# Splitting the transposed probabilities: the PSUM copy on ScalarE, the fp32r rounding on GpSimd

## The chip, the cores and the metric

The kernel runs on one core of one Trainium2 chip. The metric is the device time of one execution in microseconds (us). The kernel before has a median of 3531.86 us over 3 runs.

## The reference

A trunk of two layers over 1024 tokens of width 1024. Each layer has a token mixer (a short gated convolution beside sparse attention) and an MLP. The change lies in the attention, which has 8 query heads in 2 key groups of 4, head size 64, and three branches whose outputs are added under gates:

```python
p_cmp = masked_softmax(s_cmp, cmp_mask)          # c: 63 compressed keys
o_cmp = einsum(p_cmp, vcmp)
...
p_sel = masked_softmax(s_sel, m_sel)             # s: 8 selected blocks of 64 keys, causal
o_sel = einsum(p_sel, v_sel)
p_w = masked_softmax(s_w, m_w)                   # w: window of the last 512 keys
o_w = einsum(p_w, v_w)
o = g[:, :, 0] * o_cmp + g[:, :, 1] * o_sel + g[:, :, 2] * o_w
```

## The kernel before

Everything is float32. A product on TensorE (PE) that needs float32 accuracy is split: one operand x is written as high + low, where high is x rounded to fp32r and low = x - high, and both halves are multiplied. One Fori loop runs over the two layers, so the attention stage stands twice in the trace (about 624 to 931 us, and about 2340 to 2647 us).

**Units.** The attention runs over query tiles of 128 rows from the last (7) to the first (0). For each tile and key group there is a w set and an s set, and each set has four units, one for each head. A unit is: scores on PE into PSUM (`lin`), the negated row maximum on VectorE (DVE, `negm`, L1538), the exponential on ScalarE (ACT, L1172, into `prob`). A w set has up to 5 key tiles, an s set has all key tiles up to the diagonal (8 for the last query tile). When the four exponentials of a set are made, DVE makes four factors (`factors`, L1526 and L1528) and GpSimd (POOL) multiplies the four `prob` rows in place (L711). Between the tiles stands a c unit for the compressed branch, with a chain of some 15 small DVE instructions (L1466 to L1517).

**Groups.** Once a set is scaled, its probabilities are turned, one key tile at a time. A group is four transposes on PE (L953, L948 for the c branch) into one of the two 512-word halves ("banks") of the PSUM tile `aux`; then the split into `pTH` (high) and `pTL` (low); then `values` (L967, L968), two matmuls of 512 columns into `pv`. There are 148 such groups a layer, and 4 more of kind "b" that carry the block choice and are copied by ACT alone.

**Steps.** All engines go through one list of steps in program order, one unit a step, and no engine takes a thing out of order:

- PE at step u: the scores of the unit after this one, then the transposes of the groups of step u (two a step where the sets are long), and after each group's transposes the values of the group three places back (`V_AFTER = 3`). In a step without groups it makes the values of all groups that are waiting (a flush).
- ACT at step u: the exponential of unit u, then the high copies of step u's groups.
- DVE at step u: the maximum of unit u, then the low parts of the groups of step u - 1, then factors and the c chain where there are some.
- POOL: only the scalings, set by set.

The split of one group reads the PSUM bank twice, and it is the second read, on DVE, that frees the bank:

```python
act.activation(pt("high", x, r), turned(x, r), ACT.Copy).then_inc(t_hi, 1)                 # L1188
...
dve.tensor_tensor(pt("low", x, r), turned(x, r), pt("high", x, r).bitcast(F32),            # L1544
                  ALU.subtract).then_inc(t_free[x["bank"]], 1)
```

The transposes of a group wait on PE until the group two before it has freed the bank (L940), and `values` wait for the same semaphore (L961). `pTH` and `pTL` have four slots each (`PT = 4`): three in region r_x, the fourth in r_raw. A `region` lays several lists of tensors over one piece of SBUF.

Of the kernel before, what the change touches and what calls it, by code (L numbers as in the profile page):

```python
# [14 lines left out]
F32 = mybir.dt.float32  # L15
# [7 lines left out]
P = 128  # L23
# [197 lines left out]
PT = 4  # L221
# [5 lines left out]
def trunk(nc, a, out):  # L227

    with ExitStack() as ctx:
# [14 lines left out]
        def sem(name):  # L244
# [4 lines left out]

        other = TILE_OF[("ua", 4)] % RAW  # L250
        before = [("before", [P, other * 1024], F32)] * (other > 0)
        (wraw,), pt_r = region("r_raw", RAW * 1024, [("wraw", [P, RAW, 1024], F32)],
                               before + [("pTH3", [P, 512], F32R), ("pTL3", [P, 512], F32R)])

        (whi, wlo), (prob3,) = region("r_w", 2 * SPL * 1024, [(n, [P, SPL, 1024], F32R) for n in ("whi", "wlo")],
                                      [("prob3", [P, HPG, SEQ], F32)])
        tmp = sb("tmp", [P, 2, SEQ])


        (xT,), (cosT, sinT, kcT, vcT, fbuf, ropes), (vw, vs, pTH, pTL, scm, psum4, negm, sums, cst, imp, top8, left, fac) = region(  # L260
            "r_x", KC * SEQ, [("xT", [P, KC, SEQ], F32)],
            [("cosT", [P, SEQ], F32), ("sinT", [P, SEQ], F32), ("kcT", [P, SEQ], F32), ("vcT", [P, SEQ], F32),
             ("fbuf", [P, 2, SEQ], F32), ("ropes", [P, 2, SEQ], F32)],
# [1 line left out]
             ("pTL", [P, PT - 1, 512], F32R), ("scm", [P, NH, 64], F32), ("psum4", [P, NKV, 65], F32),  # L265
             ("negm", [P, len(UNITS) - NT], F32), ("sums", [P, len(UNITS) - NT], F32), ("cst", [P, 3, NH], F32),
             ("imp", [P, NKV, NS], F32), ("top8", [P, NKV, 8], F32), ("left", [P, NKV, NS], F32),
             ("fac", [P, 2, HPG], F32)])

        (hH, hL), (atH, atL, prob), (_, _, stG, stM), (xin,) = region(  # L270
            "r_h", 2 * KC * SEQ, [("hH", [P, KC, SEQ], F32R), ("hL", [P, KC, SEQ], F32R)],
# [62 lines left out]
        def pt(kind, x, r=P):  # L334

            t = x["v_no"] % PT
            if t == PT - 1:
                return dict(high=pt_r[-2], low=pt_r[-1])[kind][0:r, :]
            return dict(high=pTH, low=pTL)[kind][0:r, t, :]

        def turned(x, r=P):

            return aux[0:r, x["bank"] * 512:(x["bank"] + 1) * 512]

        x_keep = nc.dram_tensor("x_keep", [P, KC, SEQ], F32).ap()
        rope_keep = nc.dram_tensor("rope_keep", [2, P, SEQ], F32).ap()
# [247 lines left out]
        hid_sig, hid_silu, cmp_done, cmp_made = (sem(s) for s in ("hid_sig", "hid_silu", "cmp_done", "cmp_made"))  # L594
        rope_sum, rope_hi, v_hi, vc_lo = (sem(s) for s in ("rope_sum", "rope_hi", "v_hi", "vc_lo"))
        f_made, p_scaled = sem("f_made"), sem("p_scaled")
        t_hi, fin_low, fin_sum, fin_lo = (sem(s) for s in ("t_hi", "fin_low", "fin_sum", "fin_lo"))
        s_done, max_made, exp_made = (sem(s) for s in ("s_done", "max_made", "exp_made"))
        c_in_made, c_exp, sel_made = (sem(s) for s in ("c_in_made", "c_exp", "sel_made"))
        c_gated, t_done, v_done, o_hi = (sem(s) for s in ("c_gated", "t_done", "v_done", "o_hi"))  # L600
# [66 lines left out]
        with nc.Fori(0, DEPTH) as layer:  # L667
            with nc.Block() as block:
# [31 lines left out]
                @block.gpsimd  # L700
                def _(pool):
                    def attention():


                        for u in range(len(STEPS)):
                            for st in SETS:
                                for i in range(HPG):
                                    if st["last"] + SCALED_AFTER[i] == u:
                                        pool.wait_ge(f_made, st["no"] + 1)
                                        p = prob_of(st["no"], i)[:, 0:st["n"]]  # L710
                                        pool.tensor_scalar(p, p, fac[:, st["no"] % 2, i:i + 1], 1.0, ALU.mult, ALU.mult).then_inc(p_scaled, 1)  # L711
                                        pool.wait_ge(p_scaled, HPG * st["no"] + i + 1)

                    for n, t in enumerate(TILES):
                        if t[0] != "split":
                            continue
                        s = SPLIT_NO[n]
                        if s:

                            pool.wait_ge(w_split, s)  # L720
                        if t[5][0] == ("ua", 0):
                            attention()

                            pool.wait_ge(t_done, END_GROUP[len(SETS) - 1]["no"] + 1)
                        pool.wait_ge(raw_in[n % RAW], IN_SLOT[n])
                        if s >= SPL:

                            before = [m for m in SPLIT_NO if SPLIT_NO[m] == s - SPL][0]
                            done(pool, TILES[before][5][-1])
                        pool.tensor_scalar(whi[:, s % SPL, :], wraw[:, n % RAW, :], 1.0, 1.0, ALU.mult, ALU.mult).then_inc(w_hi, 1)  # L730
                        pool.wait_ge(w_hi, s + 1)
                        pool.tensor_tensor(wlo[:, s % SPL, :], wraw[:, n % RAW, :], whi[:, s % SPL, :].bitcast(F32),  # L732
                                           ALU.subtract).then_inc(w_split, 1)

                @block.tensor
                def _(pe):
# [219 lines left out]
                    def values(x):  # L956

                        if x["first"] and NTH[x["qt"]]:

                            pe.wait_ge(fin_sum, 2 * (NKV * (NTH[x["qt"]] - 1) + x["g"] + 1))  # L960
                        pe.wait_ge(t_free[x["bank"]], x["no"] // 2 + 1)  # L961
                        r = SEEN[x["qt"]] if x["kind"] == "c" else P
                        if x["kind"] == "c":
                            v = vcmp[0:r, x["g"], :]
                        else:
                            v = (vw if x["set"]["b"] == "w" else vs)[:, x["key"], x["g"], :]
                        pe.matmul(pv[:, x["g"], :], v, pt("high", x, r), start=x["first"], stop=False)  # L967
                        pe.matmul(pv[:, x["g"], :], v, pt("low", x, r), start=False, stop=x["last"]).then_inc(v_done, 1)  # L968
# [53 lines left out]
                def _(act):  # L1022
# [134 lines left out]
                    for u, here in enumerate(STEPS):  # L1157
                        if u < len(UNITS) and UNITS[u][0] == "c":
                            nth, n = NTH[UNITS[u][1]], SEEN[UNITS[u][1]]
                            act.wait_ge(c_in_made, nth + 1)  # L1160
                            if nth:
                                act.wait_ge(c_gated, nth)
                            act.activation(cprob[:, :, 0:n], scm[:, :, 0:n], ACT.Exp).then_inc(c_exp, 1)
                        elif u < len(UNITS):
                            b, qt, g, i, no = UNITS[u]
                            m, st = SCORES_BEFORE[u], SETS[no]
                            if no >= PROBS and i == 0:

                                act.wait_ge(t_done, END_GROUP[no - PROBS]["no"] + 1)
                            act.wait_ge(max_made, m + 1)  # L1170
                            at = chunks(st)[0][2]
                            act.activation(prob_of(no, i)[:, 0:st["n"]], scores(u)[:, at:at + st["n"]], ACT.Exp,  # L1172
                                           bias=negm[:, m:m + 1], accum_out=sums[:, m:m + 1]).then_inc(exp_made, 1)
                        for x in here:
                            o = aux[:, x["bank"] * 512:(x["bank"] + 1) * 512]
                            act.wait_ge(t_done, x["no"] + 1)
                            if x["kind"] == "b":
                                if NTH[x["qt"]] >= 2:

                                    act.wait_ge(s_done, [s for s in SETS if s["qt"] == x["qt"] + 2][-1]["last"] + 1)  # L1180
                                for g in range(NKV):
                                    ins = act.activation(selT[0:NS, x["qt"] % 2, g, :], o[32 * g:32 * g + NS, 0:P], ACT.Copy)
                                ins.then_inc(t_free[x["bank"]], 1)
                            else:
                                r = SEEN[x["qt"]] if x["kind"] == "c" else P
                                if x["v_no"] >= PT:
                                    act.wait_ge(v_done, x["v_no"] - PT + 1)
                                act.activation(pt("high", x, r), turned(x, r), ACT.Copy).then_inc(t_hi, 1)  # L1188
                        for st in SETS:
                            if st["b"] != "s":  # L1190
                                continue
                            k = NKV * NTH[st["qt"]] + st["g"]
                            if st["fin"] == u:

                                act.wait_ge(v_done, END_GROUP[st["no"]]["v_no"] + 1)
                                if k:
                                    act.wait_ge(fin_sum, 2 * k)
                                act.activation(low_half, pv[HD:P, st["g"], :], ACT.Copy).then_inc(fin_low, 1)
                            if st["fin"] + 2 == u:
                                act.wait_ge(fin_sum, 2 * (k + 1))  # L1200
                                act.activation(atH[:, 2 * st["g"]:2 * st["g"] + 2, st["qt"] * P:(st["qt"] + 1) * P],
                                               att.rearrange("p (j t) -> p j t", j=2), ACT.Copy).then_inc(o_hi, 1)
# [53 lines left out]
                def _(dve):  # L1256
# [273 lines left out]
                    for u in range(len(STEPS)):  # L1530
# [8 lines left out]
                        for x in STEPS[u - 1] if u else []:  # L1539
                            if x["kind"] != "b":  # L1540

                                r = SEEN[x["qt"]] if x["kind"] == "c" else P
                                dve.wait_ge(t_hi, x["v_no"] + 1)
                                dve.tensor_tensor(pt("low", x, r), turned(x, r), pt("high", x, r).bitcast(F32),  # L1544
                                                  ALU.subtract).then_inc(t_free[x["bank"]], 1)
                        for st in SETS:
                            if st["last"] + 1 == u:
                                factors(st)
# [164 lines left out]
```

## Time and profile before

| | |
|---|---|
| median of 3 runs | 3531.86 us (3531.05 to 3535.02) |
| time of the profiled execution | 3531.86 us |
| its span in the trace | 3530.1 us |
| busy over the span: PE, DVE, ACT, POOL | 94%, 52%, 22%, 32% |
| the low parts L1544, both layers | 296 instructions, 198.3 us, mean 686 ns |
| the scalings L711, both layers | 256 instructions, 182.6 us, mean 713 ns |

The shares are means over stages of very different kinds. Outside the attention PE works through dense products at 98 to 100% of a slice and the other engines wait for it. The attention is the part in which four engines pass work to each other, and the rows below are from there. A bracket behind an instruction in a timeline is the idle time of its engine before it, and what ended it.

### The profile page before, as it was taken

How to read it: one execution, taken by the hardware profiler on the slowest of the kernel's cores; microseconds unless marked ns; L12 is line 12 of the kernel's file. 1: busy time of each engine (PE TensorE's matmuls, PEld its weight loads, DVE VectorE, ACT ScalarE, POOL GpSimd, SP SyncE). 2: the span in 40 equal slices, each digit the busy share in tenths (PEclk: the TensorE clock that was granted, in tenths of full speed). 3: DMA queues.
4: the chain of work that ended last, by engine and by line, in shares of the span. 5: the costliest groups of instructions: out<-in, count | busy, mean ns of one | idle time of the engine just before them, and what ended most of it. 6: DMA issues, size and time to landing. Idle time of an engine off the chain costs nothing. (4 is left out here: it accounts for less than half of the span.)

```text
span 3530.1 us, 39234 instructions
## 1 busy us (share of the span) xinstructions
PE 3308.0 (94%) x15575; PEld 2687.7 (76%) x15605; DVE 1830.5 (52%) x1877; ACT 781.0 (22%) x1283; POOL 1119.9 (32%) x800
## 2 busy tenths in 40 slices
PE   4999999898898999999979999989979899999998
PEld 3788887676687888888868888767658788888887
DVE  7754344787636444333365443568865564433333
ACT  2100012666312000000120001147661210000002
POOL 3333322233332333333323333222333233333331
PEclk6999999999899999999989999999999999999999
DMA  5434431000422222111133343300005132211111
GB/s 166 147 96 131 138 96 48 1 1 1 157 66 66 72 72 68 52 48 48 36 122 96 113 137 111 81 7 1 1 9 195 37 96 72 72 48 48 48 48 60
DMA packets 349011, 256.92 MB, mean 73 GB/s; under 512 B 9500, under 2 KB 335506, under 8 KB 348563
## 3 DMA queue, kind: packets, MB, share of 16 engines
q1 hardware_dynamic: 334642, 209.75, 20.3%
q10 hardware_dynamic: 14177, 44.56, 3.4%
q8 instruction: 126, 2.06, 0.2%
q14 instruction: 66, 0.54, 0.0%
HBM read 223.87 MB, written 30.41 MB: 72 GB/s over the span
## 5 line engine op out<-in xcount | busy, mean ns | idle before, releaser
L730 POOL TENSOR_SCALAR whi<-wraw 128x1024 fp32r<-128x1024 f32 x238 | 266.2, 1119 | 1848.7 <-PE lin L759 1246.0
L759 PE MATMUL lin<-hH,whi 128*128 128x512 f32 x2272 | 719.1, 398 | 43.5 <-POOL wlo L732 35.4
L759 PE MATMUL lin<-hL,whi 128*128 128x512 f32 x2272 | 705.8, 392 | 0.0
L759 PE MATMUL lin<-hH,wlo 128*128 128x512 f32 x2272 | 705.2, 392 | 0.0
L732 POOL TENSOR_TENSOR wlo<-wraw,whi 128x1024 fp32r<-128x1024 f32 x238 | 644.2, 2707 | 19.9
L759 PEld LDWEIGHTS lin<-hH,whi 128*128 128x128 f32 x2272 | 423.9, 190 | 136.5 <-POOL wlo L732 39.5
L759 PEld LDWEIGHTS lin<-hL,whi 128*128 128x128 f32 x2272 | 430.5, 189 | 90.9
L759 PEld LDWEIGHTS lin<-hH,wlo 128*128 128x128 f32 x2272 | 429.9, 189 | 90.1
L1600 DVE SCALAR_TENSOR_TENSOR xT<-lin,adac,xT 128x1024 f32<-128x1024 f32 x144 | 184.8, 1283 | 542.3 <-PE lin L759 541.9
L711 POOL TENSOR_SCALAR prob<-prob,fac 128x640 f32<-128x640 f32 (+7 forms) x256 | 182.6, 713 | 471.2 <-DVE fac L1528 453.3
L759 PE MATMUL lin<-hidH,whi 128*128 128x512 f32 x1024 | 316.0, 390 | 0.0
L759 PE MATMUL lin<-hidL,whi 128*128 128x512 f32 x1024 | 315.5, 389 | 0.0
L759 PE MATMUL lin<-hidH,wlo 128*128 128x512 f32 x1024 | 315.5, 389 | 0.0
L1238 ACT ACTIVATE tmp<-lin 128x1024 f32<-128x1024 f32 x64 | 65.8, 1028 | 1077.6 <-PE lin L759 1076.5
L393 DVE TENSOR_REDUCE adared<-wraw 128x128 f32<-128x1024 f32 x112 | 223.3, 1993 | 94.8 <-PE pv L398 91.7
L1620 DVE TENSOR_TENSOR tmp<-tmp 128x1024 f32<-128x1024 f32 x64 | 84.0, 1313 | 352.0 <-ACT tmp L1238 352.0
L1544 DVE TENSOR_TENSOR pTL<-aux,pTH 128x512 fp32r<-128x512 f32 (+8 forms) x296 | 198.3, 686 | 50.9 <-ACT pTH L1188 49.4
L759 PEld LDWEIGHTS lin<-hidL,whi 128*128 128x128 f32 x1024 | 192.3, 188 | 39.9
L759 PEld LDWEIGHTS lin<-hidH,wlo 128*128 128x128 f32 x1024 | 192.3, 188 | 39.8
L759 PEld LDWEIGHTS lin<-hidH,whi 128*128 128x128 f32 x1024 | 191.8, 188 | 39.4
L388 DVE TENSOR_TENSOR wraw<-wraw,cT 128x1024 f32<-128x1024 f32 x112 | 201.2, 1796 | 27.3 <-DMA wraw<-in_w_ada 26.4
L1538 DVE TENSOR_REDUCE negm<-lin 128x1 f32<-128x640 f32 (+7 forms) x256 | 177.6, 703 | 37.3 <-PE lin L935 35.8
(233 smaller groups left out, 4025.5 us busy)
## 6 DMA issues: line engine op xcount, KB each, us to landing
wraw<-in_w_ff SPq DMA_DIRECT2D x128, 512.0 KB, 3.9
wraw<-in_w_ada SPq DMA_DIRECT2D x112, 512.0 KB, 4.8
wraw<-in_w_in SPq DMA_DIRECT2D x78, 512.0 KB, 3.8
x_keep<-xT SPq DMA_DIRECT2D x2, 4096.0 KB, 16.0
mix_keep<-tmp ACTq DMA_DIRECT2D x16, 512.0 KB, 2.6
gate_keep<-ropes ACTq DMA_DIRECT2D x16, 512.0 KB, 2.8
stG<-gate_keep ACTq DMA_DIRECT2D x16, 512.0 KB, 4.2
stM<-mix_keep ACTq DMA_DIRECT2D x16, 512.0 KB, 5.5
```

The source lines that it names most:

```text
L388: dve.tensor_tensor(w, w, cT[:, :].rearrange("p (k o) -> p k o", o=1).to_broadcast([P, KC, P]), ALU.mult).then_inc(ada_prod, 1)
L393: dve.tensor_reduce(adared[:, no % 2, :], w.rearrange("p k n -> p n k"), AX.X, ALU.add).then_inc(ada_used, 1)
L711: pool.tensor_scalar(p, p, fac[:, st["no"] % 2, i:i + 1], 1.0, ALU.mult, ALU.mult).then_inc(p_scaled, 1)
L730: pool.tensor_scalar(whi[:, s % SPL, :], wraw[:, n % RAW, :], 1.0, 1.0, ALU.mult, ALU.mult).then_inc(w_hi, 1)
L732: pool.tensor_tensor(wlo[:, s % SPL, :], wraw[:, n % RAW, :], whi[:, s % SPL, :].bitcast(F32), ALU.subtract).then_inc(w_split, 1)
L759: mm = pe.matmul(lin[c % 2][:, hf], w, m(k)[:, hf], start=first, stop=last)
L1238: act.activation(tmp[:, 0, :], slot(("f1", f))[:, :], ACT.Relu).then_inc(relu_made, 1)
L1538: dve.tensor_reduce(negm[:, m:m + 1], scores(u)[:, at:at + st["n"]], AX.X, ALU.max, negate=True).then_inc(max_made, 1)
L1544: dve.tensor_tensor(pt("low", x, r), turned(x, r), pt("high", x, r).bitcast(F32), ALU.subtract).then_inc(t_free[x["bank"]], 1)
L1600: dve.scalar_tensor_tensor(out=xT[:, i, :], in0=slot(name)[:, :], scalar=adac[:, gate + i:gate + i + 1], in1=xT[:, i, :], op0=ALU.mult, op ...
L1620: dve.tensor_tensor(tmp[:, 1, :], tmp[:, 0, :], tmp[:, 0, :], ALU.mult).then_inc(hid_sq, 1)
```

## The change

ACT now copies the turned group from PSUM into SBUF as plain float32 (`pTF`), and that copy frees the bank. POOL rounds `pTF` to `pTH`. DVE subtracts `pTH` from `pTF` and writes `pTL`, both inputs now in SBUF; `pTF` lies on the same memory as `pTL`, so the subtraction is in place. `values` wait for the new semaphore `t_lo`. In POOL's program the roundings of step u stand ahead of the scalings of step u, which are now spread over the steps in the order of the loop; after each rounding POOL waits for its own `t_hi`. Nothing else is changed, and no memory is added.

```diff
-        (wraw,), pt_r = region("r_raw", RAW * 1024, [("wraw", [P, RAW, 1024], F32)],
-                               before + [("pTH3", [P, 512], F32R), ("pTL3", [P, 512], F32R)])
+        (wraw,), pt_r, pt_f = region("r_raw", RAW * 1024, [("wraw", [P, RAW, 1024], F32)],
+                                     before + [("pTH3", [P, 512], F32R), ("pTL3", [P, 512], F32R)],
+                                     [(n + "_", sh, dt) for n, sh, dt in before] + [("pTH3_", [P, 512], F32R), ("pTF3", [P, 512], F32)])
...
-                return dict(high=pt_r[-2], low=pt_r[-1])[kind][0:r, :]
-            return dict(high=pTH, low=pTL)[kind][0:r, t, :]
-
-        def turned(x, r=P):
-
-            return aux[0:r, x["bank"] * 512:(x["bank"] + 1) * 512]
+                return dict(high=pt_r[-2], low=pt_r[-1], both=pt_f[-1])[kind][0:r, :]
+            return dict(high=pTH, low=pTL, both=pTF)[kind][0:r, t, :]
...
-                        for u in range(len(STEPS)):
+                        for u, here in enumerate(STEPS):
+                            for x in here:
+                                if x["kind"] != "b":
+                                    r = SEEN[x["qt"]] if x["kind"] == "c" else P
+                                    pool.wait_ge(t_free[x["bank"]], x["no"] // 2 + 1)
+                                    pool.tensor_scalar(pt("high", x, r), pt("both", x, r), 1.0, 1.0, ALU.mult, ALU.mult).then_inc(t_hi, 1)
+                                    pool.wait_ge(t_hi, x["v_no"] + 1)
                             for st in SETS:
                                 for i in range(HPG):
                                     if st["last"] + SCALED_AFTER[i] == u:
...
-                        pe.wait_ge(t_free[x["bank"]], x["no"] // 2 + 1)
+                        pe.wait_ge(t_lo, x["v_no"] + 1)
...
-                                act.activation(pt("high", x, r), turned(x, r), ACT.Copy).then_inc(t_hi, 1)
+                                act.activation(pt("both", x, r), o[0:r, :], ACT.Copy).then_inc(t_free[x["bank"]], 1)
...
-                                dve.tensor_tensor(pt("low", x, r), turned(x, r), pt("high", x, r).bitcast(F32),
-                                                  ALU.subtract).then_inc(t_free[x["bank"]], 1)
+                                dve.tensor_tensor(pt("low", x, r), pt("both", x, r), pt("high", x, r).bitcast(F32),
+                                                  ALU.subtract).then_inc(t_lo, 1)
```

## Rows read from the trace of the kernel before

**Rows 1.** Stretches: length, busy PE, PEld, DVE, ACT, POOL (instructions), clock, DMA, GB/s.

```profile
640.00:820.00 180.00, 165.07 (x1031) 125.92 (x1044) 151.33 (x289) 123.17 (x250) 56.76 (x64) 1.00 0.00 1
820.00:931.00 111.00, 89.64 (x529) 65.88 (x529) 77.22 (x194) 69.83 (x191) 39.00 (x68) 0.93 0.01 3
2356.30:2536.30 180.00, 165.16 (x1031) 126.02 (x1044) 151.05 (x287) 122.86 (x250) 56.75 (x64) 1.00 0.00 1
```

**Rows 2.** Who waited for whom, 640 to 931 us: total us, times, longest.

```profile
PEld aux L953 <- DVE pTL L1544: 23.4, 33, 2.0
PE aux L953 <- DVE pTL L1544: 17.2, 27, 1.7
PEld pv L967 <- DVE pTL L1544: 15.9, 19, 2.3
PE pv L967 <- DVE pTL L1544: 9.4, 8, 2.2
```

**Rows 3.** Timeline of PE behind the c chain, at 666 us.

```profile
666.32 0.66 PE L953 MATMUL aux<-ident,prob 128*128 128x128 f32 x4 [1.50 <-DVE pTL L1544]
```

**Rows 4.** The pTL instructions alone, by stretch.

```profile
640.00:820.00 180.00, 64.16 (x96) 1.00 0.00 1
```

**Rows 5.** Instructions by line and shape, 640 to 970 us: POOL, then DVE.

```profile
L711 POOL TENSOR_SCALAR prob<-prob,fac 128x512 f32<-128x512 f32 x16 | 11.3, 708 | 24.4 <-DVE fac L1528 23.3
L711 POOL TENSOR_SCALAR prob<-prob,fac 128x1024 f32<-128x1024 f32 x8 | 9.0, 1121 | 18.7 <-DVE fac L1528 18.1
L730 POOL TENSOR_SCALAR whi<-wraw 128x1024 fp32r<-128x1024 f32 x5 | 5.2, 1046 | 25.7 <-PE lin L759 24.2 <-PE aux L953 1.4
```
```profile
L1544 DVE TENSOR_TENSOR pTL<-aux,pTH 128x512 fp32r<-128x512 f32 x132 | 88.3, 687 | 19.4 <-ACT pTH L1188 18.7
```

**Rows 6.** Single lines, min/median/max ns: DVE with both inputs in SBUF; POOL.

```profile
L1569 DVE TENSOR_TENSOR atL<-tmp,atH x32: 414/418/594, 685.3 to 2646.0; 128x256 fp32r<-128x256 f32 x32
...
L1585 DVE TENSOR_TENSOR mxL<-tmp,mxH x16: 1212/2318/3430, 947.3 to 2697.6; 128x1024 fp32r<-128x1024 f32 x16
...
L732 POOL TENSOR_TENSOR wlo<-wraw,whi x238: 2342/2398/3840, 88.9 to 3482.5; 128x1024 fp32r<-128x1024 f32 x119
```

**Rows 7.** Timeline, 946 to 955 us: POOL, then DVE.

```profile
946.16 3.46 POOL L732 TENSOR_TENSOR wlo<-wraw,whi 128x1024 fp32r<-128x1024 f32 x1
```
```profile
946.13 1.23 DVE L1582 TENSOR_TENSOR tmp<-tmp,stM 128x1024 f32<-128x1024 f32 x1
947.27 3.43 DVE L1585 TENSOR_TENSOR mxL<-tmp,mxH 128x1024 fp32r<-128x1024 f32 x1
```

**Rows 8.** DVE by shape, 640 to 970 us: same shapes, POOL busy or not.

```profile
L1486 DVE TENSOR_TENSOR tmp<-tmp,cst 128x376 f32<-128x376 f32 x1 | 1.1, 1114 | 0.0
L1486 DVE TENSOR_TENSOR tmp<-tmp,cst 128x440 f32<-128x440 f32 x1 | 1.0, 995 | 0.0
L1489 DVE TENSOR_TENSOR tmp<-tmp 128x312 f32<-128x312 f32 x1 | 0.9, 879 | 0.0
...
L1489 DVE TENSOR_TENSOR tmp<-tmp 128x440 f32<-128x440 f32 x1 | 0.6, 616 | 0.0
L1489 DVE TENSOR_TENSOR tmp<-tmp 128x376 f32<-128x376 f32 x1 | 0.6, 551 | 0.0
...
L1486 DVE TENSOR_TENSOR tmp<-tmp,cst 128x312 f32<-128x312 f32 x1 | 0.5, 483 | 0.0
```

**Rows 9.** Timeline, 697 to 700 us: POOL, then DVE.

```profile
697.69 4.34 POOL L711 TENSOR_SCALAR prob<-prob,fac 128x896 f32<-128x896 f32 x4 [8.67 <-DVE fac L1528]
```
```profile
698.23 0.69 DVE L1544 TENSOR_TENSOR pTL<-aux,pTH 128x512 fp32r<-128x512 f32 x1
699.13 0.69 DVE L1544 TENSOR_TENSOR pTL<-aux,pTH 128x512 fp32r<-128x512 f32 x1 [0.21 <-ACT pTH L1188]
```

**Rows 10.** Timeline of PE in a flush, at 914 us.

```profile
914.49 0.50 PE L967 MATMUL pv<-pTH,vw 128*128 128x512 f32 x1 [2.17 <-DVE pTL L1544]
```

**Rows 11.** Timeline of POOL: the scalings of one set of 1024 keys.

```profile
648.07 4.77 POOL L711 TENSOR_SCALAR prob<-prob,fac 128x1024 f32<-128x1024 f32 x4 [3.75 <-DVE fac L1528]
```

More of the change, by code:

```diff
@@ L257, in trunk @@
         tmp = sb("tmp", [P, 2, SEQ])
-        (xT,), (cosT, sinT, kcT, vcT, fbuf, ropes), (vw, vs, pTH, pTL, scm, psum4, negm, sums, cst, imp, top8, left, fac) = region(
+        (xT,), (cosT, sinT, kcT, vcT, fbuf, ropes), (vw, vs, pTH, pTL, scm, psum4, negm, sums, cst, imp, top8, left, fac), (_, _, _, pTF) = region(
             "r_x", KC * SEQ, [("xT", [P, KC, SEQ], F32)],
@@ L267, in trunk @@
              ("imp", [P, NKV, NS], F32), ("top8", [P, NKV, 8], F32), ("left", [P, NKV, NS], F32),
-             ("fac", [P, 2, HPG], F32)])
+             ("fac", [P, 2, HPG], F32)],
+            [("vw_", [P, NT, NKV, P], F32R), ("vs_", [P, NT, NKV, P], F32R), ("pTH_", [P, PT - 1, 512], F32R),
+             ("pTF", [P, PT - 1, 512], F32)])
         (hH, hL), (atH, atL, prob), (_, _, stG, stM), (xin,) = region(
@@ L596, in trunk @@
         f_made, p_scaled = sem("f_made"), sem("p_scaled")
-        t_hi, fin_low, fin_sum, fin_lo = (sem(s) for s in ("t_hi", "fin_low", "fin_sum", "fin_lo"))
+        t_hi, t_lo, fin_low, fin_sum, fin_lo = (sem(s) for s in ("t_hi", "t_lo", "fin_low", "fin_sum", "fin_lo"))
         s_done, max_made, exp_made = (sem(s) for s in ("s_done", "max_made", "exp_made"))
```

## The prediction

> **What bounds the kernel now.** I read the page's slices first. Outside the attention PE is at 98 to 100% of nearly every slice, and the change touches nothing there, so only the two attention stages can move. The busy time by stretch splits one stage into a dense part of 180 us (640 to 820, long sets, two groups a step) and a sparse part of 111 us (820 to 931, short sets) [rows 1]. In the dense part PE is busy for 165.1 us (92%) and DVE for 151.3 us (84%): two engines are near their limit, and DVE has 28.7 us of idle time left. ACT has 123.2 us, POOL only 56.8 us. In the sparse part nobody is full (PE 81%, DVE 70%). The second layer repeats this (165.2 and 151.1 us), so I work out one layer and double it. The table of waits says what keeps PE from its work [rows 2]: transposes that wait for the low part, because it frees the bank, 23.4 us a layer by the weight loads (17.2 us by the matmuls); values that wait for the low part, 15.9 us (9.4 us). The timeline shows the first kind: after the c chain DVE is late with two low parts, and the transposes stand still for 1.50 us [rows 3].
>
> **What is removed.** The bank is now freed by ACT's copy, so a transpose no longer waits for DVE's read. The rows allow at most 23.4 us a layer for that, 47 us in all. PE does not get it all: it still waits for DVE through `values`, only later. Before, the transposes of group n needed the low part of group n - 2; now they stand in PE's program behind the values of group n - 4. DVE may be four groups late instead of two.
>
> **ACT** does one copy of one bank as before, only the output type differs. I cost it at nothing; ACT is at 68%, so some ns more on each would be hidden.
>
> **POOL** gets 148 roundings a layer, 96 of them in the dense part (as many as low parts there) [rows 4]. The shape 128x512 to fp32r is not in the trace. The same instruction at 1024 elements takes 1046 ns, and the scaling takes 1121 ns at 1024 and 708 ns at 512, so 512 elements less are worth 413 ns [rows 5]: 1046 - 413 = 633 ns. Bounds: half of 1046, that is 523 ns, and 708 ns. POOL's dense part becomes 56.8 + 96 x 0.63 = 117 us of 180, or 65%. The wait for its own semaphore costs what lies between the scalings of a set: 4.77 us for four of 1.121 leave 0.29 us in three gaps, some 0.09 us each [rows 5, 11]. POOL is no bound by itself. Behind a rounding that waits for ACT stand the scalings of that step. They are due at steps 1, 2 and 3 after the set's last unit and are read by transposes at step 5; at 2.5 to 3 us a step (two groups a step, 96 groups in 180 us) two steps hold the last two scalings (2.2 us) and a pair of roundings (1.4 us), so I cost this move at nothing. If that cover went, PE would wait up to some 0.5 us a set, 8 us in both layers.
>
> **DVE** keeps its instruction but reads two SBUF tensors. Undisturbed, 256 elements take 414 ns and 1024 take 1212 ns [rows 6], so 512 lie at 414 + 798/3 = 680 ns, which is what it takes now from PSUM (687 ns) [rows 5]. Nothing is saved there. What changes is who disturbs it. A DVE instruction with both inputs in SBUF and a POOL instruction exclude each other: `tmp` starts at 946.13 and POOL's `wlo` at 946.16, and `wlo` takes 3.46 us where its median is 2.40; `mxL`, whose least is 1.21 us, starts at 947.27, while `wlo` is under way, and ends at 950.70, 1.08 us after `wlo` [rows 6, 7]. The same pairing happens in the attention: the c chain's instructions take 1114 instead of 551 ns, 995 instead of 616, 879 instead of 483 when a scaling runs beside them [rows 8], on average 0.45 us more; the smallest excess in this stage is that of one `atL`, 594 instead of 414 ns [rows 6], or 0.18 us. A low part meets short roundings as often as long scalings, so I take a value near the middle of the two, 0.34 us for a meeting. The low part as it is now, with one input in PSUM, is not disturbed: 0.69 us twice beside four scalings in 4.34 us [rows 9].
>
> The Trainium skill states this (SBUF — State Buffer, Who interferes with whom): a Vector instruction with two SBUF inputs contends with a GpSimd instruction that reads SBUF, the pair of ports is an exclusive lock for the whole instruction, and one with a single SBUF input does not contend. The trace agrees on both halves. Taken strictly, with every instruction holding the lock for its whole length, it leads to the second rival below instead of my sum.
>
> So each of the 96 low parts pays 0.34 us x the share of time in which POOL works, 0.65: 0.22 us. Bounds: 0.1 us (only half the meetings cost, or POOL finds its gaps) and 0.4 us (low part and POOL's next instruction wake on the same semaphore, so they meet nearly always).
>
> **The sum, dense part.** DVE: 151.3 + 96 x 0.22 = 172.4, and some 1.5 us for the c chain and `atL`, which meet POOL more often: 174 us of work in a part that lasted 180. DVE becomes the bound. Its idle time was 28.7 us; with four groups of slack instead of two I let it keep a third, 9.6 us. 174 + 9.6 = 183.6 us, against 180: +3.6 us. So the 23.4 us of bank waits do go away, but PE then waits for the low part in `values`.
>
> **The sum, sparse part.** In a flush PE waits for the group just turned, 2.17 us in the row shown [rows 10]. That chain gets one link more, 0.63 + 0.09 = 0.72 us. Where three groups are flushed, the third's transposes were held up by the bank, and that returns about as much as the link costs. By the kernel's plan six of the last ten flushes hold one or two groups and get nothing back: 6 x 0.72 = 4.3 us. A little of the bank waits between them is won, some 0.5 us: +3.8 us.
>
> Both: +7.4 us a layer, +15 us in all. The profiled execution took 3531.86 us (its span of 3530.1 and 1.8 us around it), which is also the median, so I predict **3547 us**.
>
> **Rivals.**
> - *The deeper slack wins (faster).* If a meeting costs 0.1 us, DVE has 151.3 + 9.6 + 1 = 162 us of work; with 5 us idle it needs 167 us, and PE with 165.1 us is the bound again at about 168: -12 us in the dense part, +2 in the sparse one, -20 us in all: **3512 us**. For it: half the waits of PE are on the bank, and while DVE is late, POOL works ahead of it. It decides below about 0.17 us a low part. Against it: DVE starts at 84%.
> - *The lock is the bound (much slower).* POOL and the low parts in the dense part are 56.8 + 96 x (0.63 + 0.69) = 183.5 us, and with the c chain's and `atL`'s some 188 us, in 180 us. In-order engines do not pack without gaps; with a tenth of gaps 207 us: +27, and +8 in the sparse part where every flush pays, +70 us in all: **3602 us**. Against it: `mxL` ends 1.08 us after `wlo` although it is 1.21 us long by itself, so part of each instruction overlaps.
> - *Nothing moves.* Bank waits won and meetings paid cancel: within 7 us of 3532. DVE's idle time would only have to shrink to 6 us.
>
> **Chances.** A measurement of this kernel tells about 0.2% (7 us) from no change. My forecast (3540 to 3565) 0.40; the deeper slack 0.30; nothing moves 0.17; the lock 0.13. So faster 0.30, same 0.17, slower 0.53. The range takes in the forecast, no change, the centre of the faster case and the lower part of the lock case: 3508 to 3590.
>
> **What the profile after would show.** Transposes (L953) that wait for the low part are gone, and those that wait for ACT are short. The low part's mean is 0.85 to 0.95 us instead of 0.687 (right if over 0.8; the faster rival if under 0.8; the lock if over 1.05). Roundings at 0.6 to 0.7 us when alone. DVE busy 93% or more from 640 to 820. More wait of PE for `pTL` in L967 than 15.9 us a layer. What would make it wrong: ACT's copy to plain float32 of another length, a DVE that gets the port at once while POOL's instruction pays, which spares the engine that is full, or PE waiting for scalings that come late.

## The result, and the profile after

The changed kernel takes 3650.7 us (median of 4 runs, 3644.67 to 3652.62) against 3531.66 us (3531.05 to 3535.02): a ratio of 1.033, with an interval of 1.032 to 1.035. It is slower by 119 us where 15 us were forecast, outside the range.

The page of the kernel after, its costliest groups. They answer to the lines of the low parts and the scalings in the table before and in [rows 5]: line, engine, instruction, count, busy us and mean ns, then idle time before it.

```profile
L709 POOL TENSOR_SCALAR pTH<-pTF 128x512 fp32r<-128x512 f32 (+8 forms) x296 | 219.2, 740 | 277.4 <-ACT pTF L1193 263.2
...
L1549 DVE TENSOR_TENSOR pTL<-pTF,pTH 128x512 fp32r<-128x512 f32 (+8 forms) x296 | 208.3, 717 | 144.4 <-POOL pTH L709 144.3
...
L716 POOL TENSOR_SCALAR prob<-prob,fac 128x640 f32<-128x640 f32 (+7 forms) x256 | 248.6, 971 | 29.5 <-DVE fac L1533 5.4
```

The low part on DVE has hardly changed (717 ns, 686 before), but DVE now stands idle for 144 us ahead of it. The scalings on POOL, whose code is the same, take 971 ns instead of 713. Both point one way: where the two engines meet, it is mostly POOL that pays. The first experiment tests it.

The marks of POOL's timeline after show where in the stage the time went: the first scaling of all, the first one of 512 elements, and the first dense weight behind the attention.

```profile
645.82 3.48 POOL L716 TENSOR_SCALAR prob<-prob,fac 128x640 f32<-128x640 f32 x4 [1.17 <-DVE fac L1533]
...
857.22 1.19 POOL L716 TENSOR_SCALAR prob<-prob,fac 128x512 f32<-128x512 f32 x1
...
990.26 1.54 POOL L735 TENSOR_SCALAR whi<-wraw 128x1024 fp32r<-128x1024 f32 x1
```

The same marks of the kernel before:

```profile
640.84 3.48 POOL L711 TENSOR_SCALAR prob<-prob,fac 128x640 f32<-128x640 f32 x4 [43.41 <-DVE fac L1528]
...
820.27 3.05 POOL L711 TENSOR_SCALAR prob<-prob,fac 128x512 f32<-128x512 f32 x4 [4.37 <-DVE fac L1528]
...
926.27 1.04 POOL L730 TENSOR_SCALAR whi<-wraw 128x1024 fp32r<-128x1024 f32 x1 [1.39 <-PE aux L953]
```

The dense part grew from 179.4 to 211.4 us (+32), the sparse part from 106.0 to 133.0 us (+27), in one layer. The second layer is alike. That the sparse part, where no engine is full, lost nearly as much is the first hint that a full engine is not the whole cause.

Busy time by stretch after, columns as in [rows 1]:

```profile
645.00:855.00 210.00, 178.45 (x1031) 129.62 (x1046) 159.88 (x287) 120.79 (x248) 145.36 (x159) 0.96 0.00 1
855.00:990.00 135.00, 100.58 (x523) 71.63 (x521) 81.19 (x192) 69.09 (x189) 87.62 (x116) 0.88 0.00 1
```

DVE is busy for 159.9 of 210 us, or 76% where it was 84%; it is not the bound. POOL has 69% and 65%.

PE is busy longer over the same work. In the dense part the same 1031 matmuls take 178.5 us instead of 165.1, and in the sparse part 100.6 us instead of 89.6; the granted clock is 0.96 and 0.88 where it was 1.00 and 0.93 [rows 1]. Of the 54 us by which the two stretches are longer, PE is busy for 24 and idle for 30. One place where the clock goes down, in the dense part: PE has just waited 2.24 us for a low part, and in the 3.4 us after that the granted clock is 0.50 (1.2 instead of 2.4 GHz) and PE is busy all the time with 12 matmuls.

```profile
731.48 0.50 PE L972 MATMUL pv<-pTH,vs 128*128 128x512 f32 x1 [2.24 <-DVE pTL L1549]
```
```profile
732.00:735.40 3.40, 3.40 (x12) 2.30 (x12) 3.12 (x14) 0.94 (x2) 2.52 (x4) 0.50 0.00 0
```

So a wait of PE was followed here by slower matmuls, and the loss is more than the wait. Over the whole execution PE is busy for 3362.0 us instead of 3308.0, 54 us more: at most that is what the lower clock costs PE directly. No run changes the clock by itself, so how much of the 119 us it makes is not shown.

Who waited for whom after, 640 to 1000 us (total us, times, longest):

```profile
ACT prob L1177 <- DVE negm L1543: 98.9, 73, 4.1
DVE pTL L1549 <- POOL pTH L709: 72.8, 85, 4.2
PEld pv L972 <- DVE pTL L1549: 58.5, 57, 2.9
...
PE aux L958 <- POOL prob L716: 11.2, 16, 1.7
```

and two lines of the kernel before, 640 to 931 us, beside those in [rows 2]:

```profile
ACT prob L1172 <- DVE negm L1538: 34.2, 38, 2.2
DVE pTL L1544 <- ACT pTH L1188: 25.0, 60, 3.1
```

The transposes no longer wait for the low part, as the change meant. In its place `values` wait for it 58.5 us a layer (15.9 before), DVE waits for POOL 72.8 us (25.0 for ACT before), and since DVE takes nothing out of order, the maxima behind the low part are late and the exponentials wait 98.9 us (34.2 before).

How the pair of engines takes turns is seen in two timelines of the kernel after, 701 to 704 us, POOL and then DVE:

```profile
701.89 0.81 POOL L709 TENSOR_SCALAR pTH<-pTF 128x512 fp32r<-128x512 f32 x1 [0.39 <-ACT pTF L1193]
702.81 1.29 POOL L716 TENSOR_SCALAR prob<-prob,fac 128x640 f32<-128x640 f32 x1
```
```profile
701.54 0.69 DVE L1549 TENSOR_TENSOR pTL<-pTF,pTH 128x512 fp32r<-128x512 f32 x1 [0.32 <-POOL pTH L709]
702.74 0.69 DVE L1549 TENSOR_TENSOR pTL<-pTF,pTH 128x512 fp32r<-128x512 f32 x1 [0.51 <-POOL pTH L709]
```

The first low part runs from 701.54 to 702.23. The second rounding starts on paper at 701.89 and takes 0.81 us instead of its usual 0.62: it ends 0.47 us after the low part. The second low part, which needs it, waits 0.51 us and starts 0.04 us after its end; POOL's next instruction, which waits for the same event, starts 0.11 us after it, finds the port taken, and takes 1.29 us. Before, a scaling of this shape took 0.81 us on average, from 640 to 970 us:

```profile
L711 POOL TENSOR_SCALAR prob<-prob,fac 128x640 f32<-128x640 f32 x40 | 32.4, 810 | 100.6 <-DVE fac L1528 97.7
```

So this pair of groups runs rounding, low, rounding, low, nearly one after the other. It is not so in every pair: of the 296 roundings in the trace 91 took over 0.68 us, and of the 296 low parts 26 took over 0.72 us. The spans of POOL are the rough ones in a profile, so a difference of a few hundredths of a us is given as it is read and proves little.

### The profile page after: what moved, and what is told of

Same layout as the page of the kernel before. It is cut to its first block and busy times, and to the rows that moved or that the text cites. A ratio compares the mean times of both kernels' runs of the same rounds, so it can differ in the third digit from the quotient of the medians.

```text
span 3653.8 us, 39829 instructions
## 1 busy us (share of the span) xinstructions
PE 3362.0 (92%) x15575; PEld 2708.2 (74%) x15605; DVE 1855.4 (51%) x1877; ACT 778.1 (21%) x1283; POOL 1398.6 (38%) x1096
## 5 line engine op out<-in xcount | busy, mean ns | idle before, releaser
L737 POOL TENSOR_TENSOR wlo<-wraw,whi 128x1024 fp32r<-128x1024 f32 x238 | 636.6, 2675 | 19.9
L709 POOL TENSOR_SCALAR pTH<-pTF 128x512 fp32r<-128x512 f32 (+8 forms) x296 | 219.2, 740 | 277.4 <-ACT pTF L1193 263.2
L1549 DVE TENSOR_TENSOR pTL<-pTF,pTH 128x512 fp32r<-128x512 f32 (+8 forms) x296 | 208.3, 717 | 144.4 <-POOL pTH L709 144.3
L716 POOL TENSOR_SCALAR prob<-prob,fac 128x640 f32<-128x640 f32 (+7 forms) x256 | 248.6, 971 | 29.5 <-DVE fac L1533 5.4
L1177 ACT ACTIVATE prob<-lin,negm 128x640 f32<-128x640 f32 (+7 forms) x256 | 178.9, 699 | 214.1 <-DVE negm L1543 211.0
```

Of the source, the lines that this page charges most:

```text
L709: pool.tensor_scalar(pt("high", x, r), pt("both", x, r), 1.0, 1.0, ALU.mult, ALU.mult).then_inc(t_hi, 1)
L1549: dve.tensor_tensor(pt("low", x, r), pt("both", x, r), pt("high", x, r).bitcast(F32), ALU.subtract).then_inc(t_lo, 1)
```

## The experiments

Every time is set against runs of the kernel before that were taken beside it (medians 3533.41, 3536.50, 3530.81 and 3534.57 us for the four groups of experiments); "+50.9" is the difference of the two medians. The interval of each is some 3 to 7 us to either side, so differences between two experiments are good to a few us.

**One SBUF input for the low part.** An edit of the changed kernel.

```diff
-dve.tensor_tensor(pt("low", x, r), pt("both", x, r), pt("high", x, r).bitcast(F32),
-                  ALU.subtract).then_inc(t_lo, 1)
+dve.tensor_reduce(pt("low", x, r), pt("both", x, r).rearrange("p (n o) -> p n o", o=1), AX.X,
+                  ALU.max).then_inc(t_lo, 1)
```

> The changed kernel, with DVE's subtraction replaced by a maximum over an axis of one element: same place, same waits, 512 elements from pTF alone, so one SBUF input instead of two (the low part is then not the difference). Theory 1 (the two-input subtraction and POOL hinder each other, and POOL pays): the roundings fall from 740 to about 620 ns and the scalings from 971 to about 713 ns, the second rounding of a pair no longer waits for the first low part, and most of the 119 us is given back: 3550 to 3590 us. Theory 2 (the extra link itself, whatever the engines do to each other): roundings and scalings get shorter all the same, but the time stays over 3620 us.

Measured: 3584.35 us, +50.9, ratio 1.015 (1.013 to 1.017). POOL and DVE of this kernel, 640 to 990 us:

```profile
L1549 DVE TENSOR_REDUCE pTL<-pTF 128x512 fp32r<-128x512 f32 (+7 forms) x148 | 98.9, 680 | 47.5 <-POOL pTH L709 46.8
L709 POOL TENSOR_SCALAR pTH<-pTF 128x512 fp32r<-128x512 f32 (+7 forms) x148 | 92.8, 627 | 149.9 <-ACT pTF L1193 143.4 <-DVE fac L1533 2.2
L716 POOL TENSOR_SCALAR prob<-prob,fac 128x640 f32<-128x640 f32 (+7 forms) x128 | 92.5, 723 | 15.2 <-DVE fac L1533 3.1
```

The low part has the same length (680 ns), and with its second SBUF input gone the roundings are back at 627 and the scalings at 723 ns. That input is worth 119.0 - 50.9 = 68 us. The time is in theory 1's range, but theory 1 holds for a little more than half of the loss; the rest is something else.

**Scalings of 4 columns.** The changed kernel; most probabilities are left unscaled.

```diff
-p = prob_of(st["no"], i)[:, 0:st["n"]]
+p = prob_of(st["no"], i)[:, 0:4]
```

> The changed kernel, with each scaling on POOL cut to the first 4 columns of its row; the rest of the probabilities stays unscaled, all waits stay. Theory 1 (port between the subtraction and POOL): scalings no longer matter, but the pairs rounding against low part stay, so a part comes back, 30 to 60 us: 3590 to 3620 us. Theory 3 (POOL is simply full in the dense part, 145 of 210 us busy, and roundings queue behind scalings): nearly all of the loss in the dense part, 60 us in both layers, comes back, the sparse part keeps its 54: about 3590 us or less. Theory 2 (link): little, over 3630 us.

Measured: 3607.88 us, +74.5, ratio 1.021 (1.020 to 1.023). 44.5 us come back, in theory 1's range. POOL being full is not the cause: with its scalings nearly gone the kernel is still 74.5 us slower than before.

**Both edits together.**

> The first two together: one SBUF input for the low part and scalings of 4 columns. What stays of the change is the early free bank and a rounding of 0.62 us in the chain. Theory 1: 3520 to 3560 us, close to the run with one input alone. Theory 3: clearly below that run, by 20 us or more. Theory 2: still over 3600 us.

Measured: 3570.93 us, +37.5, ratio 1.011 (1.009 to 1.013). With one input, the scalings are worth only 13.4 us (50.9 - 37.5), against 44.5 us with two: most of their price is meeting low parts, not POOL's time. Where little but the roundings can meet a low part, the second input is worth 74.5 - 37.5 = 37.0 us, and the roundings take 738 ns with it (the run with scalings of 4 columns) and 628 ns without. The run came out some 10 us above theory 1's range, so a rounding in the chain by itself costs more than I had thought.

**The link alone, in the kernel before.** POOL rounds 4 columns again between ACT and DVE.

```diff
+for x in here:
+    if x["kind"] != "b":
+        pool.wait_ge(t_hi, x["v_no"] + 1)
+        pool.tensor_scalar(pt("high", x, r)[:, 0:4], pt("high", x, r)[:, 0:4].bitcast(F32), 1.0, 1.0, ALU.mult, ALU.mult).then_inc(t_lnk, 1)
+        pool.wait_ge(t_lnk, x["v_no"] + 1)
...
-dve.wait_ge(t_hi, x["v_no"] + 1)
+dve.wait_ge(t_lnk, x["v_no"] + 1)
```

> The kernel before, with one step put between ACT's copy and DVE's low part: POOL rounds 4 columns of pTH again, in the place where the changed kernel does its roundings, and waits for itself; DVE waits for POOL. Bank, DVE's PSUM input and all lengths are those of before. Theory 2 (the link and the order on POOL): slower by 60 us or more, since the bank also waits for the link. Theory 1: the link alone is short (0.2 to 0.3 us a group) and costs 10 to 40 us: 3540 to 3570 us.

Measured: 3560.91 us, +27.5, ratio 1.008 (1.006 to 1.009), as theory 1 had it. A link of 0.2 us (mean 196 ns) with POOL's waits around it costs 27.5 us when the bank waits for it too.

**The early bank alone.** ACT writes pTH and frees the bank; no work of POOL between; the low part is a maximum over one element of pTH, so it is not the difference.

```diff
-(the roundings on POOL)
-act.activation(pt("both", x, r), o[0:r, :], ACT.Copy).then_inc(t_free[x["bank"]], 1)
+act.activation(pt("high", x, r), o[0:r, :], ACT.Copy).then_inc(t_free[x["bank"]], 1)
...
-dve.wait_ge(t_hi, x["v_no"] + 1)
+dve.wait_ge(t_free[x["bank"]], x["no"] // 2 + 1)
```

> Only the early free bank: ACT's copy makes pTH and frees the bank, POOL makes no roundings and does its scalings set by set as before, and DVE's low part is a maximum over an axis of one element, read from pTH alone (so it is not the difference). Theory A (freeing the bank at ACT's copy is worth something, and the link then costs more than the 51 us that stayed without the port): faster than before, 3500 to 3520 us. Theory B (PE only waits for the low part in another place): within 7 us of before, and the link costs the 51 us.

Measured: 3519.07 us, -17.4, ratio 0.995 (0.994 to 0.996). Theory A. The waits of this kernel, 635 to 1000 us:

```profile
PEld pv L966 <- DVE pTL L1543: 25.7, 33, 2.3
...
PEld aux L952 <- ACT pTH L1187: 1.5, 3, 0.5
```

Of the 23.4 us in front of the transposes 1.5 are left, and `values` wait for 9.8 us more than the 15.9 of [rows 2]. The early bank is real and small, 9 us a layer.

**The same with two SBUF inputs** (pTH subtracted from itself, so the low part is zero).

> The run with the early bank alone, with the low part as a subtraction of pTH from itself: two SBUF inputs, and POOL has only the scalings, in bursts of four. If DVE's two-input instructions cost only while POOL is in the same chain, the scalings get longer (up to 0.8 us each time a low part falls into one) but the time stays within 10 us of the run with one input. If meeting the scalings is itself costly, 20 us or more are added.

Measured: 3536.69 us, +0.2, ratio 1.000 (0.999 to 1.001). 17.6 us more than with one input: between the two cases that were expected. Meeting the scalings alone eats up the whole gain of the early bank. Nothing that DVE waits for is on POOL here, and POOL pays even so: the scalings grow from 719 to 965 ns, the low part from 679 to 752 ns.

**The short link with the early bank.** The run with the early bank alone, with POOL's rounding put back on 4 columns of pTH in place, in the changed kernel's order.

> The run with the early bank alone, and POOL between ACT's copy and the low part again, but with 4 columns (0.2 us) instead of 512: one SBUF input for the low part, scalings in full, and in the changed kernel's order. Against it stands the run with one input and full roundings (3584 us). If the length of the rounding makes the link dear: near 3540 us, as the link put into the kernel before cost 27 us. If the order on POOL (scalings standing between the roundings) does it: near 3570 us.

Measured: 3534.35 us, +3.5, ratio 1.001 (1.000 to 1.002). The short link costs 20.9 us (3.5 + 17.4), and making it long, 0.62 instead of 0.20 us, costs 47.4 us (50.9 - 3.5). So most of it is the length of the rounding; the place among the scalings is already in the 20.9 us.

**The short link with two SBUF inputs.**

> The run with the short link (4 columns on POOL, the early bank, 3534 us), with the low part as a subtraction of pTH from itself, so two SBUF inputs. POOL has almost no rounding that could collide, but the scalings are as in the changed kernel. If the 66 us of the two inputs come from roundings and low parts that take turns (rounding, low, rounding, low), most of it is missing here: 3545 to 3560 us. If they come from low parts that fall into scalings: 3585 to 3600 us.

Measured: 3565.12 us, +30.6, ratio 1.008 (1.007 to 1.010), just above the first case. The second input costs 27.1 us here (30.6 - 3.5), nearly all from the scalings, which take 977 ns on the page (728 with the short link and one input), and 68.1 us with roundings of full length. The other 41 us need long roundings beside the low parts. The 37.0 us found above, where little but roundings could meet a low part, give the same share from the other side. That it comes about by the taking of turns is read from the timelines above.

**Both halves on ACT.** The full computation: ACT copies the bank twice, the second copy frees it.

> The full computation without POOL in the chain: ACT makes pTH from the bank, then pTF from the bank, which frees it; DVE subtracts from SBUF. ACT gets 148 copies of 0.6 us a layer more, 89 us on top of 193 in a stage of 291 (123 + 57 = 180 of 180 us in the dense part). ACT full: 3560 to 3600 us. If its idle time in front of the transposes takes them in: 3520 to 3540 us.

Measured: 3587.29 us, +50.8, ratio 1.014 (1.013 to 1.016), in the first case's range.

**Both halves on DVE.** The full computation: DVE rounds `pTF` to `pTH` and subtracts.

> The full computation, with ACT's copy to pTF freeing the bank and DVE making both halves from SBUF; POOL only has the scalings. DVE gets 148 more instructions a layer. At 0.3 to 0.4 us each the dense part's DVE goes from 151 to some 185 us of 180: 3550 to 3600 us. At 0.6 us each 209 us: 3600 to 3650 us. In both cases over the kernel before, which would show that a fourth pass over the turned group has no free engine.

Measured: 3697.26 us, +166.5, ratio 1.047 (1.045 to 1.049). The rounding took 455 ns on average, 67 us a layer, and the low part 841 ns. It came out above both cases, so the count of busy time sized this one too low as well.

**The low part ahead of the maximum.** The kernel before, only DVE's order within a step changed.

```diff
 for u in range(len(STEPS)):
+    (low parts of the groups of step u - 1)
     if u < len(UNITS):
         dve.wait_ge(s_done, u + 1)
         ...
-    (low parts of the groups of step u - 1)
```

> The kernel before, only DVE's order changed: in each step the low parts of the step before stand ahead of the maximum. The bank is freed up to 0.8 to 1.2 us earlier in program order. If the bank wait of 23 us a layer matters, faster by 10 to 30 us; if DVE then stands and waits for ACT's copy while the maximum could run, and the exponential comes later, slower by 20 us or more. It shows what a DVE that waits at the head of its queue costs.

Measured: 3669.44 us, +132.9, ratio 1.037 (1.036 to 1.039). No instruction was added, and the low parts, maxima and scalings have their length of before (686, 694 and 708 ns). PE is busy for 3366.5 us instead of 3308.0: here too part of the loss is longer matmuls. The waits, 635 to 1000 us:

```profile
ACT prob L1172 <- DVE negm L1545: 132.4, 98, 3.4
DVE pTL L1536 <- ACT pTH L1188: 114.1, 86, 5.0
```

This is the same picture as in the changed kernel, made by order alone: a DVE that waits at the head of its queue makes the exponentials late.

**The low part two steps later.** The changed kernel in full, `STEPS[u - 2]` in place of `STEPS[u - 1]` in DVE's loop.

> The changed kernel in full, with one edit: DVE makes the low parts of a step two steps later instead of one, so that POOL has a step more before DVE stands and waits for it. If the way of the loss is DVE at the head of its queue, which makes the maximum, the exponential and the scores late, DVE's wait for POOL falls from 73 us a layer to under 20 and much comes back: 3560 to 3610 us. If the loss is in PE's values, which need the low part, it gets worse, 3700 us or more, since the low part is made later.

Measured: 3671.68 us, +140.9, ratio 1.039 (1.037 to 1.041). The waits, 635 to 1020 us:

```profile
PEld pv L972 <- DVE pTL L1549: 82.2, 67, 3.9
...
DVE pTL L1549 <- POOL pTH L709: 24.7, 27, 4.2
```

DVE's wait for POOL fell from 72.8 to 24.7 us, near what was expected, and the kernel got slower by another 22 us all the same: `values` now wait for 82.2 us. My theory that the head of DVE's queue is the one way of the loss falls. A late low part costs either way: it lands on the maxima or on the values. The run is not a clean test of that alone. A low part no longer starts right behind its rounding, and now DVE pays more: 813 ns a low part instead of 717, and 894 ns a scaling instead of 971.

## Why the prediction was wrong

The whole 119.0 us, built up one difference at a time over five kernels. The terms add up to it by their making, and the size of each depends on the order: the second input is worth 17.6 us where POOL makes no roundings, and 68.1 us as the last step.

| step | kernels | us |
|---|---|---|
| bank freed by ACT's copy | early bank alone, to before | -17.4 |
| a short link on POOL | short link, to early bank alone | +20.9 |
| the rounding at full length | one SBUF input, to short link | +47.4 |
| the second SBUF input | changed kernel, to one SBUF input | +68.1 |

- **What is removed.** Right in kind: the bank waits are gone and part of them turns up in `values`. The forecast gave the early bank no price of its own; it is 17.4 us.
- **ACT's copy at nothing, POOL's rounding at 633 ns, the low part undisturbed at 680 ns.** Right: ACT's copy still has a median of 597 ns, the rounding 618 ns, the low part 691 ns.
- **"each of the 96 low parts pays 0.34 us x the share of time in which POOL works".** This step failed. The mechanism, DVE and POOL hindering each other, was right, and the share of meetings was near (68 of 95 low parts of the dense part ran beside an instruction of POOL, 72% where 65% was forecast); but I charged them to DVE. Its low part grew by 31 ns, not 220. POOL paid: its roundings grew from 627 to 738 ns and its scalings from 723 to 973 ns a layer when the second input came in. By the prediction's own sign a low part under 0.8 us spoke for the faster rival; it took 0.717 us, and the kernel was slower all the same. The prediction named this case ("a DVE that gets the port at once while POOL's instruction pays") and took it for good news, as it "spares the engine that is full". But POOL had just been put ahead of DVE in the chain, so what POOL loses, DVE waits for. In [rows 8] DVE was the loser, with a scaling already under way; but the first pair of [rows 7] showed the other side, `tmp` at 1.23 us and POOL's `wlo` at 3.46 us, and the price was taken from DVE's excess alone. In the chain DVE is awake 0.04 us after the rounding and POOL 0.11 us after it. The Trainium skill (SBUF — State Buffer, Who interferes with whom) states that the one that starts first has the pair for the whole instruction. These two timelines agree up to 0.15 us: the rounding that was held up ended 0.47 us after the low part, where it takes 0.62 us by itself.
- **"DVE becomes the bound."** Failed with it: DVE's share of the dense part fell to 76%.
- **The link, in the dense part.** Nothing was charged, on the ground of four groups of slack; in the sparse part 4.3 us a layer. Measured, link and full rounding cost 68.3 us in both layers (20.9 + 47.4) without any second input. The mis-sized term is this one as much as the first. The slack of PE is not slack of DVE: DVE makes the low parts of step u - 1 right behind the maximum of step u, and before the change it already waited for the copy 60 times a layer, 25.0 us over 148 low parts, as in [rows 9]. For those 0.72 us more had no cover.
- **Scalings moved at nothing.** Too low: transposes wait for scalings for 11.2 us a layer after, where at most 8 us in both layers was allowed for; with one input it is 1.7 us, so the move itself costs little and the longer scalings make the rest.
- **PE at its 165.1 us.** Every sum and rival holds PE's work fixed, with no reason given. It grew by 24 us a layer in the two stretches, at a lower granted clock. This is a share of the steps above, not one beside them: the more a run lost, the more PE was busy (3308.0 us before, 3314.3 with the short link, 3331.7 with one input, 3362.0 in the changed kernel).
- **The rivals.** None was right. The lock rival had the larger size and the right resource (3602 us), but its cause, a port that is full, is not what was measured: with the scalings at 4 columns 74.5 us of the loss remain, and with one input 50.9 us.

Why 0.42 us more of rounding (125 us over 296 groups) come out as 47 us of time was not taken apart further. The two waits in which the delay lands are shown; how it splits over flushes and full steps, and how much of it is PE at the lower clock, stays open. That DVE wins the port because it wakes first was read from the timelines and not tried by itself. Two runs bear on it: with the low part two steps later DVE pays more and the scalings less, which speaks for it; but with the early bank and two inputs POOL wakes nobody and pays most all the same, so it is not the whole reason.

Neither a version with the halves on ACT nor one with them on DVE beats the kernel before, and the early bank alone, which leaves the difference out, gains 0.5%.

## What to carry to other kernels

When two engines share a resource, ask not only how long they meet but which of them is ahead in the chain: what the one upstream loses, the one downstream waits for. A step put between two engines that already run at each other's heels is paid in latency even where every engine has idle time, so look at the small regular waits (0.2 us before an instruction, many times over) for the sign that there is no cover. And do not hold PE's time fixed when its waits grow: look at the granted clock beside them. A free buffer handed back earlier is worth only what is left when the next wait, here that of the values, takes over.

## What the hardware showed that was not expected

- In the changed kernel a low part with two SBUF inputs nearly keeps its length (717 ns against 686) while the scalings beside it grow by a third (723 to 973 ns). Where it is not woken by POOL it pays too: 752 ns with the early bank, 813 ns two steps later. The idle column shows nothing of this, since the wait is inside the duration.
- In the one meeting shown, POOL's instruction overlapped the low part a little: the rounding ended 0.47 us after it, where 0.62 us is its length alone.
- Behind a wait of PE the granted clock fell to 0.50 for 3.4 us; over the whole execution PE was busy 54 us longer with the same products.
- 4 columns on POOL take 196 ns, 512 take 618 ns; a step of 4 columns between ACT and DVE costs 21 to 28 us over 296 groups.
- Putting the low parts ahead of the maximum in DVE's order, with no other edit, cost 133 us.
